# Value pages multiplied four at a time instead of two, with the loads, the v and u weights and the sample's scan products regrouped

## The chip, the core and the metric

The kernel runs on one core of a Trainium2 chip. The metric is the device time of one execution in microseconds (us). In the rows, PE is the matrix engine (TensorE), PEld its weight loads, DVE the vector engine, ACT the scalar engine, POOL GpSimd, SP the sync engine whose queue issues most of the loads.

## What is computed

One decoder layer for a prompt of 256 tokens and for 8 samples with one new token each, so 264 columns go through every product together. One projection `z = x @ w_in` feeds two mixers, differential attention and a diagonal state-space scan; their outputs are projected, gated, merged and go through `w_out`, a layer norm and a gated MLP. Cut to what the change touches:

```python
z = x @ w_in                          # q, k, v, u, gate_a, gate_s
k_past = cache_k[l][page_table].reshape(bs, n_pages * PAGE_SIZE, N_HEADS, 2, HEAD_DIM)
v_past = cache_v[l][page_table].reshape(bs, n_pages * PAGE_SIZE, N_HEADS, V_DIM)
...
s = jnp.einsum('bqhjd,bkhjd->bhjqk', q, k) * (HEAD_DIM ** -0.5)
p = jax.nn.softmax(s, axis=-1)
p_diff = p[:, :, 0] - lam * p[:, :, 1]
return jnp.einsum('bhqk,bkhe->bqhe', p_diff, v)
...
bu_re = jnp.einsum('blgc,gpc->blgp', ug, bb_re)      # scan inputs
y = jnp.einsum('blgp,gcp->blgc', x_re, c_re) - jnp.einsum('blgp,gcp->blgc', x_im, c_im)
```

Each sample has 2048 past tokens: 16 pages of keys and 16 of values, 128 tokens to a page, 512 KB each. With 8 samples this is 128 pages of each kind.

## The kernel before

All of `z` is made on PE as fp32 products, a 128 x 128 block of `w_in` against 264 columns (the matmul in `z_group`, L740). A tile of `z` is one bank of 128 outputs and takes 16 such matmuls; each shows as two records in the trace, so "x16" there is eight matmuls. Tiles q, k, v, u, g (gates) and glu follow the list `GROUPS`: most in pairs that share a load of 1 MB in rows of 1024 B, a few alone, in rows of 512 B. ACT issues these loads into a ring of four places and takes every finished tile from its bank (L1241).

Everything else of the attention and the scan is hung between those matmuls. There are seven *rounds* `i` = 0 to 6 that go over the tiles v, u and four g (round 6 has no u). A *quarter* is four matmuls of z; a round has 24 quarters (round 6 has 20), and the dictionary `at` names what PE does ahead of a quarter:

- `scores` (L858), `max_rows`, `global_max` (L896), `denominators` (L901), `combine` (L909), the transposes to rows (L689) and `prompt_pv` (L884, L885) are small products for the attention of prompt head `i` and sample `i`;
- `outputs_and_inputs` are the prompt's scan products `bu` (L832, 32-row tiles of the array) and `cx` (L843);
- `page_pv` (L720) multiplies one page of values: four matmuls with 16 columns of weights each, at four column groups of the array, against 256 columns of the page. Sixteen pages accumulate in one bank. In the kernel before they go two at a time (`pages_pv(i, 0, 1)` and so on), at quarters 2, 5, 10, 12, 15, 17, 20 and 23;
- `sample_bu` (L952) and `sample_cx` (L962) are the samples' scan products, 16 matmuls of 32 columns each.

For the keys, POOL multiplies each page with the query (L648), DVE reduces it (L1793); DVE also does maxima, the scan's states and the softmax parts. K pages have five places in memory, V pages four. SP issues the page loads, each after it has read the page's number (L453, L454), in the order of one list; it stops at a page whose place isn't free, with all that is behind it in the list.

`MAIL_ORDER` fixes the order in which small results pass from PE through one bank to ACT (`post` on PE, `take` on ACT). After the rounds come g 28 and 29, eight glu tiles and g 30 and 31, with sample 7's pages, the states' transposes and the mean squares of the norms in between. Then the weights of the remaining layers are split in two parts, high by ACT (L1487) and low by DVE (L1955), and multiplied as three products (L1083, L1084, L1089), first for the two branch projections and so on to the end. That part is not touched but for two waits.

## Time and profile before

| | |
|---|---|
| timed runs | 1684.76, 1690.97, 1694.06 us; median 1690.97 us |
| profiled execution | 1686.51 us, its span 1684.7 us |
| PE busy | 1642.8 us, 98% of the span |
| DVE, ACT, POOL busy | 1128.9, 647.8, 388.9 us |
| HBM traffic | 385.24 MB read, 5.46 MB written, 232 GB/s over the span |
| first projection product | 696.02 us after the start of the span |

The four middle rounds each take 61.80 us, round 5 (486.3 to 552.0 us) 65.7 us. In the rows an instruction's start and duration stand with its line; durations on PE overlap, since matmuls are pipelined, so what a run of matmuls costs is read from one start to the next. "[0.27 <-ACT ...]" is idle time before an instruction and what ended it.

### The profile page before, as it was taken

The page shows a single profiled execution, that of the slowest core. Times are in us where ns is not written, and L with a number is a line of the kernel's source. Part 1 is how long each engine was busy: PE and PEld are TensorE (multiplying, and loading weights), DVE is VectorE, ACT ScalarE, POOL GpSimd, SP SyncE. Part 2 cuts the span into 40 slices and gives each one's busy share as a digit, 9 for nine tenths or more (in the row PEclk, how much of TensorE's full clock was granted, in tenths as well). Part 3 has the DMA queues.
Part 4 walks back from the last instruction along what each step waited for, and adds up shares of the span by engine and source line. Part 5 has one row for each costly group of instructions (what it writes and reads, how often), then busy time and mean ns, then how long its engine had stood idle before and what let it go on. Part 6 is the DMA issues. An engine that isn't in the chain of part 4 may idle for free. (4 is left out here: it accounts for less than half of the span.)

```text
span 1684.7 us, 31240 instructions
## 1 busy us (share of the span) xinstructions
PE 1642.8 (98%) x11730; PEld 1466.0 (87%) x11730; DVE 1128.9 (67%) x1748; ACT 647.8 (38%) x979; POOL 388.9 (23%) x341
## 2 busy tenths in 40 slices
PE   9999999999999899899997999999999999999996
PEld 7878777777777676899997999999999999999995
DVE  2382897897888943777667767777777775545555
ACT  2121343443443322333347444444444443333333
POOL 1066587687677610000001000000000000000001
PEclk9999999999999999999998999999999999999998
DMA  9679899999999968666663676666766666666651
GB/s 251 213 229 312 285 392 387 388 394 386 388 392 394 327 230 260 166 182 180 186 177 99 186 192 173 178 179 180 192 174 176 182 178 168 183 180 179 183 152 53
DMA packets 484439, 391.81 MB, mean 233 GB/s; under 512 B 23550, under 2 KB 448411, under 8 KB 484316
## 3 DMA queue, kind: packets, MB, share of 16 engines
q1 hardware_dynamic: 401388, 323.27, 62.4%
q10 hardware_dynamic: 82944, 67.11, 12.8%
q8 instruction: 67, 1.10, 0.3%
q14 instruction: 40, 0.33, 0.1%
HBM read 385.24 MB, written 5.46 MB: 232 GB/s over the span
## 5 line engine op out<-in xcount | busy, mean ns | idle before, releaser
L740 PE MATMUL bank<-work,weight_ring 128*128 128x264 f32 x2176 | 518.2, 393 | 0.5 <-ACT work L1205 0.5
L1487 ACT ACTIVATE weights_hi<-weight_ring 128x2048 fp32r<-128x2048 f32 (+1 forms) x166 | 309.8, 1866 | 512.8 <-PE bank L1084 395.6
L740 PEld LDWEIGHTS bank<-work,weight_ring 128*128 128x128 f32 x2176 | 406.9, 192 | 91.3 <-issue 24.3
L1955 DVE TENSOR_TENSOR weights_lo<-weight_ring,weights_hi 128x2048 fp32r<-128x2048 f32 (+1 forms) x166 | 369.1, 2224 | 112.6 <-ACT weights_hi L1487 67.2
L1083 PE MATMUL bank<-h_hi,weights_hi 128*128 128x264 f32 x1344 | 330.9, 284 | 0.0
L1084 PE MATMUL bank<-h_lo,weights_hi 128*128 128x264 f32 x1344 | 330.1, 284 | 0.0
L648 POOL TENSOR_TENSOR work<-work 128x512 f32<-128x512 f32 x256 | 317.7, 1278 | 37.1 <-DMA work<-toeplitz_rows 20.7
L678 POOL TENSOR_TENSOR work<-work,ffn_scratch 128x1056 f32<-128x1056 f32 x4 | 9.5, 2406 | 1058.0 <-ACT ffn_scratch L1205 1058.0
L1083 PEld LDWEIGHTS bank<-h_hi,weights_hi 128*128 128x128 f32 x1344 | 253.2, 188 | 0.0
L1084 PEld LDWEIGHTS bank<-h_lo,weights_hi 128*128 128x128 f32 x1344 | 252.7, 188 | 0.0
L1793 DVE TENSOR_REDUCE work<-work 128x8 f32<-128x512 f32 x256 | 165.2, 677 | 52.6 <-POOL work L648 52.1
L1089 PE MATMUL bank<-h_hi,weights_lo 128*128 128x264 f32 x1344 | 176.5, 284 | 0.0
L1083 PE MATMUL bank<-hidden_hi,weights_hi 128*128 128x264 f32 x688 | 171.1, 286 | 1.8 <-DVE ffn_scratch L2083 1.8
L1084 PE MATMUL bank<-hidden_lo,weights_hi 128*128 128x264 f32 x688 | 170.7, 286 | 0.0
L1089 PEld LDWEIGHTS bank<-h_hi,weights_lo 128*128 128x128 f32 x1344 | 168.4, 188 | 0.0
L1205 ACT ACTIVATE work<-bank 128x264 f32<-128x264 f32 (+9 forms) x117 | 39.6, 352 | 263.4 <-PE bank L689 92.7
L1083 PEld LDWEIGHTS bank<-hidden_hi,weights_hi 128*128 128x128 f32 x688 | 130.6, 190 | 2.0 <-DVE ffn_scratch L2083 2.0
L1084 PEld LDWEIGHTS bank<-hidden_lo,weights_hi 128*128 128x128 f32 x688 | 130.5, 190 | 0.0
L2080 DVE SCALAR_TENSOR_TENSOR ffn_scratch<-bank,conv_and_ln_parameters,ffn_scratch 128x255 f32<-128x255 f32 x86 | 41.5, 483 | 126.4 <-ACT ffn_scratch L1205 126.4
L1089 PE MATMUL bank<-hidden_hi,weights_lo 128*128 128x264 f32 x688 | 91.4, 284 | 0.0
L1089 PEld LDWEIGHTS bank<-hidden_hi,weights_lo 128*128 128x128 f32 x688 | 86.7, 188 | 0.0
L637 POOL TENSOR_SCALAR work<-work 128x256 f32<-128x256 f32 x32 | 34.5, 1077 | 178.3 <-ACT work L1266 178.3
(272 smaller groups left out, 1939.5 us busy)
## 6 DMA issues: line engine op xcount, KB each, us to landing
weight_ring<-in_w_up SPq DMA_DIRECT2D x86, 1024.0 KB, 5.6
work<-in_cache_k SPq DMA_DIRECT2D x128, 512.0 KB, 7.0
work<-in_cache_v SPq DMA_DIRECT2D x128, 512.0 KB, 7.3
weight_ring<-in_w_in ACTq DMA_DIRECT2D x60, 1024.0 KB, 14.7
weight_ring<-in_w_down SPq DMA_DIRECT2D x32, 1024.0 KB, 5.9
weight_ring<-in_w_out SPq DMA_DIRECT2D x16, 1024.0 KB, 5.9
weight_ring<-in_w_down SPq DMA_DIRECT2D x16, 704.0 KB, 4.8
weight_ring<-in_w_proj_attn SPq DMA_DIRECT2D x16, 512.0 KB, 4.2
```

Of the source, the lines that this page charges most:

```text
L637: ch.did(pool.tensor_scalar(whole_turns, turns, 1.5 * 2 ** 23, -1.5 * 2 ** 23, ALU.add, ALU.add))
L648: pool.tensor_tensor(half_page(2 * n + e), half_page(2 * n + e), q_b[b % 2][:, e * 512:(e + 1) * 512], ALU.mult).then_inc(kq_ready, 1)
L678: pool.tensor_tensor(c3, c3, mean_y.unsqueeze(1).to_broadcast([P, 4, N]), ALU.subtract).then_inc(cent_ready, 1)
L740: last = pe.matmul(bank[(n + m) % 2][:, 0:N], chunk_weight(g, k - c * per, m), tiles[k], start=(k == 0), stop=(k == len(tiles) - 1))
L1083: pe.matmul(dst[:, 0:N], weight(w_hi, off, k0 + k), highs[k], start=start and k == 0, stop=False)
L1084: last = pe.matmul(dst[:, 0:N], weight(w_hi, off, k0 + k), lows[k], start=False, stop=False)
L1089: last = pe.matmul(dst[:, 0:N], weight(w_lo, off, k0 + k), highs[k], start=False, stop=stop and k == len(highs) - 1)
L1205: return act.activation(dst, src, ACT.Copy, scale=scale)
L1487: act.activation(w_hi[:, (j % 2) * KT * P:(j % 2) * KT * P + k_tiles * P].bitcast(F32R), slot3(j, 0, k_tiles).rearrange("p k m -> p (k m)" ...
L1793: dve.tensor_reduce(score[b % 3][:, p * 16 + 8 * e:p * 16 + 8 * e + 8], half_page(2 * n + e).rearrange("p (m d) -> p m d", d=HD), AX.X, AL ...
L1955: dve.tensor_tensor(w_lo[:, cols].bitcast(F32R), slot3(off % SLOTS, 0, k_tiles).rearrange("p k m -> p (k m)"), w_hi[:, cols], ALU.subtract ...
L2080: n1 = ch.did(dve.scalar_tensor_tensor(y[:, 1:T], ps[:, 0:T - 1], par(1), y[:, 1:T], ALU.mult, ALU.add))
```

## The change

Values: the 64 bursts of two pages become 32 of four, at quarters 10, 15, 20 and, in the next round, 4. SP's list is regrouped to match: V loads stand four together, K loads between them. `combine` moves from quarter 12, ahead of `denominators`, to behind the pages of quarter 15.

Weights: in rounds 0 to 5 the tiles v of two rounds make one pair and so do the tiles u, so twelve single loads become pairs; `v_t` gets a second place.

Samples: `sample_bu`, once 16 matmuls in one run at quarter 16 of round 6, goes in four parts of four matmuls at quarters 13 to 16, and `sample_cx`, once at quarter 1 after round 6, in four parts at quarters 17 to 20 of it, now into bank 4. DVE's mask of u and its read of the result move with them.

End of the input projection: `combine` of sample 7, the samples' mean square and the two transposes of states change places inside the last group, and PE's and DVE's waits before the first projection are split, so that g 31 is awaited only at the second product group and the stores only at the first merge.

```diff
+ROUNDS = []
+for _i in range(0, H - 2, 2):
+    ROUNDS += [[(("v", _i + 1), ("v", _i + 2)), (("u", _i + 2), ("u", _i + 3)), (("g", 4 * _i), ("g", 4 * _i + 1))],
+               in_pairs("g", 4 * _i + 2, 4 * _i + 8)]
+ROUNDS += [[(("v", H - 1),), *in_pairs("g", 4 * H - 8, 4 * H - 4)]]
...
-                for what in ("Sk", "P14", "P15", "V0", "K5", "V1", "K6", "Sv", "V2", "K7", "V3", "Bias", "K8", "Q", "V4", "K9",
-                             "V5", "K10", "V6", "K11", "V7", "V8", "K12", "V9", "K13", "V10", "K14", "V11", "K15", "V12",
-                             "N0", "N1", "V13", "N2", "N3", "N4"):
+                for what in ("Sk", "K5", "K6", "Sv", "V0", "V1", "V2", "V3", "K7", "Bias", "K8", "Q", "K9",
+                             "V4", "V5", "V6", "V7", "K10", "K11", "K12", "V8", "V9", "V10", "V11", "K13", "K14", "K15",
+                             "V12", "V13", "V14", "V15", "N0", "N1", "N2", "N3", "N4"):
...
-            def pages_pv(b, *numbers):
-                for p in numbers:
+            def pages_pv(b, first):
+                for p in range(first, first + 4):
                     if b >= 0:
                         page_pv(b, p)
...
-            def sample_bu():
-                pe.wait_ge(um_ready, 1)
-                pe.wait_ge(sc_read, 2 * (H - 1))
-                for t in range(HT):
+            def sample_bu(t0):
+                if t0 == 0:
+                    pe.wait_ge(um_ready, 1)
+                    pe.wait_ge(sc_read, 2 * (H - 1))
+                for t in range(t0, t0 + 2):
...
-                at = {2: lambda: (values_to_rows(i), pages_pv(i - 1, 12, 13)),
+                at = {2: lambda: values_to_rows(i),
                       3: lambda: max_rows(i),
-                      4: lambda: scores(i, 1, 1),
-                      5: lambda: (global_max(i), pages_pv(i - 1, 14, 15)),
+                      4: lambda: (scores(i, 1, 1), pages_pv(i - 1, 12)),
+                      5: lambda: global_max(i),
                       8: lambda: outputs_and_inputs(t, 0),
-                      10: lambda: (scores(i, 0, 0), pages_pv(i, 0, 1)),
+                      10: lambda: (scores(i, 0, 0), pages_pv(i, 0)),
                       12: lambda: diagonal_scores_and_sums(i)}
                 if whole:
-                    at |= {15: lambda: pages_pv(i, 4, 5),
-                           17: lambda: pages_pv(i, 6, 7),
-                           20: lambda: (pages_pv(i, 8, 9), outputs_and_inputs(t, 2)),
+                    at |= {15: lambda: (pages_pv(i, 4), combine_of(i - 1)),
+                           20: lambda: (pages_pv(i, 8), outputs_and_inputs(t, 2)),
                            21: lambda: p_diff_rows(i),
-                           23: lambda: (pages_pv(i, 10, 11), keys_to_rows(i + 1))}
+                           23: lambda: keys_to_rows(i + 1)}
                 else:
-                    at |= {14: lambda: pages_pv(i, 4, 5),
-                           16: lambda: (pages_pv(i, 6, 7), sample_bu()),
-                           18: lambda: pages_pv(i, 8, 9),
-                           20: lambda: (pages_pv(i, 10, 11), outputs_and_inputs(t, 2))}
+                    at |= {13: lambda: sample_bu(0),
+                           14: lambda: (pages_pv(i, 4), combine(i - 1), sample_bu(2)),
+                           15: lambda: sample_bu(4),
+                           16: lambda: sample_bu(6),
+                           17: lambda: sample_cx(0),
+                           18: lambda: (sample_cx(2), pages_pv(i, 8)),
+                           19: lambda: (p_diff_rows(i), sample_cx(4)),
+                           20: lambda: (sample_cx(6), outputs_and_inputs(t, 2), keys_to_rows(i + 1))}
+                z_groups(ROUNDS[i], at)
...
             z_group((("g", 30), ("g", 31)),
-                    {2: states_out, 4: sample_states_out, 5: lambda: combine(B - 1)})
-            pe.wait_ge(sq_ready, 2)
-            pe.matmul(bank[5][:, 0:H * B], v_mean_w[:, :], sq_sample, start=True, stop=True).then_inc(ms_done, 1)
+                    {1: lambda: combine(B - 1), 4: sample_mean_square, 5: states_out, 7: sample_states_out})
...
-            pe.wait_ge(z_read, PROJ0)
+            pe.wait_ge(z_read, PROJ0 - 1)
+            pe.wait_ge(mail_read, len(MAIL_ORDER))
```

How PE's order changes, in matmuls (line numbers of the changed kernel are one lower here). Before, on PE in the middle of a round, from the second scores product of quarter 10 on: L720 are pages, L740 is z, L909 `combine`, L901 `denominators`.

```order
L858 MATMUL bank<-work 128x128
L720 MATMUL bank<-work 16x256 x8
L740 MATMUL bank<-work,weight_ring 128x264 x8
L720 MATMUL bank<-work 16x256 x8
L858 MATMUL bank<-work 128x128
L909 MATMUL bank<-small,work 128x4 x2
L901 MATMUL bank<-work,ones 128x32
L740 MATMUL bank<-work,weight_ring 128x264 x12
L720 MATMUL bank<-work 16x256 x8
L740 MATMUL bank<-work,weight_ring 128x264 x8
L720 MATMUL bank<-work 16x256 x8
```

In the changed kernel the same stretch, pages on L719, z on L739, `combine` on L908, `denominators` on L900:

```order
L857 MATMUL bank<-work 128x128
L719 MATMUL bank<-work 16x256 x16
L739 MATMUL bank<-work,weight_ring 128x264 x8
L857 MATMUL bank<-work 128x128
L900 MATMUL bank<-work,ones 128x32
L739 MATMUL bank<-work,weight_ring 128x264 x12
L719 MATMUL bank<-work 16x256 x16
L908 MATMUL bank<-small,work 128x4 x2
L739 MATMUL bank<-work,weight_ring 128x264 x20
L719 MATMUL bank<-work 16x256 x16
```

Two bursts of eight page matmuls with z between have become one of sixteen, and `combine` has left the place ahead of `denominators` and stands behind the next pages.

PE in round 6 before, around `sample_bu` (L952):

```order
L740 MATMUL bank<-work,weight_ring 128x264 x8
L720 MATMUL bank<-work 16x256 x8
L740 MATMUL bank<-work,weight_ring 128x264 x8
L720 MATMUL bank<-work 16x256 x8
L952 MATMUL bank<-work 128x32 x16
L740 MATMUL bank<-work,weight_ring 128x264 x8
L720 MATMUL bank<-work 16x256 x8
L740 MATMUL bank<-work,weight_ring 128x264 x8
```

PE in round 6 of the changed kernel, `sample_bu` on L952 and `sample_cx` on L962:

```order
L739 MATMUL bank<-work,weight_ring 128x264 x4
L952 MATMUL bank<-work 128x32 x4
L739 MATMUL bank<-work,weight_ring 128x264 x4
L719 MATMUL bank<-work 16x256 x16
L908 MATMUL bank<-small,work 128x4 x2
L952 MATMUL bank<-work 128x32 x4
L739 MATMUL bank<-work,weight_ring 128x264 x4
L952 MATMUL bank<-work 128x32 x4
L739 MATMUL bank<-work,weight_ring 128x264 x4
L952 MATMUL bank<-work 128x32 x4
L739 MATMUL bank<-work,weight_ring 128x264 x4
L962 MATMUL bank<-work 128x32 x4
```

The run of 16 small matmuls has become four runs of four, each with z work of a quarter behind it; `sample_cx` follows in the same way.

PE in the last group before the projections (g 30, g 31), before: L689 the transposes of states, L1073 the samples' mean square, L1083 the first projection product.

```order
L740 MATMUL bank<-work,weight_ring 128x264 x8
L689 MATMUL bank<-ident,work 32x128 x2
L740 MATMUL bank<-work,weight_ring 128x264 x8
L689 MATMUL bank<-ident,work 128x128 x4
L740 MATMUL bank<-work,weight_ring 128x264 x4
L909 MATMUL bank<-small,work 128x4 x2
L740 MATMUL bank<-work,weight_ring 128x264 x12
L1073 MATMUL bank<-work,v_mean_w 128x64
L1083 MATMUL bank<-att_hi,weights_hi 128x264
```

The same in the changed kernel (L688, L908, L1071, L1084):

```order
L739 MATMUL bank<-work,weight_ring 128x264 x4
L908 MATMUL bank<-small,work 128x4 x2
L739 MATMUL bank<-work,weight_ring 128x264 x12
L1071 MATMUL bank<-work,v_mean_w 128x64
L739 MATMUL bank<-work,weight_ring 128x264 x4
L688 MATMUL bank<-ident,work 32x128 x2
L739 MATMUL bank<-work,weight_ring 128x264 x8
L688 MATMUL bank<-ident,work 128x128 x4
L739 MATMUL bank<-work,weight_ring 128x264 x4
L1084 MATMUL bank<-att_hi,weights_hi 128x264
```

The mean square now has three quarters of z and both transposes behind it; it was the last thing ahead of the projections.

## Rows read from the trace of the kernel before

**Rows 1.** The page: span; PE busy us and its share of the span

```profile
span 1684.7 us, 31240 instructions
...
PE 1642.8 (98%) x11730; PEld 1466.0 (87%) x11730; DVE 1128.9 (67%) x1748; ACT 647.8 (38%) x979; POOL 388.9 (23%) x341
```

**Rows 2.** By windows: busy us of PE, PEld, DVE, ACT, POOL; clock, DMA, GB/s

```profile
424.50:486.30 61.80, 61.53 (x381) 44.39 (x380) 51.34 (x86) 25.60 (x56) 46.73 (x41) 1.00 1.05 389
486.30:552.00 65.70, 61.69 (x381) 44.36 (x381) 55.27 (x84) 25.24 (x54) 45.37 (x40) 1.00 1.03 383
552.00:625.00 73.00, 70.47 (x429) 51.32 (x429) 46.01 (x81) 19.51 (x40) 34.81 (x29) 0.91 0.79 278
```

**Rows 3.** Timeline of PE, a round: start us, duration us, line, records

```profile
505.55 0.61 PE L909 MATMUL bank<-small,work 128*128 128x4 f32 x4
506.43 0.41 PE L901 MATMUL bank<-work,ones 128*128 128x32 f32 x2 [0.27 <-ACT work L1205]
...
512.19 1.06 PE L720 MATMUL bank<-work 128*16 128x256 f32 x16
513.18 3.83 PE L740 MATMUL bank<-work,weight_ring 128*128 128x264 f32 x16
516.93 1.06 PE L720 MATMUL bank<-work 128*16 128x256 f32 x16
517.92 5.61 PE L740 MATMUL bank<-work,weight_ring 128*128 128x264 f32 x24
...
536.79 3.73 PE L740 MATMUL bank<-work,weight_ring 128*128 128x264 f32 x16
540.35 0.38 PE L689 MATMUL bank<-ident,work 128*128 128x128 f32 x2
...
552.00 0.36 PE L896 MATMUL bank<-small,ones 16*128 16x16 f32 x2 [3.74 <-DVE small L1810]
```

**Rows 4.** Timeline of PE, around the sample's scan products

```profile
584.40 0.63 PE L720 MATMUL bank<-work 128*16 128x256 f32 x8 [0.57 <-DMA work<-in_cache_v]
584.95 4.67 PE L952 MATMUL bank<-work 128*128 128x32 f32 x32
589.44 6.26 PE L740 MATMUL bank<-work,weight_ring 128*128 128x264 f32 x16
...
607.45 3.66 PE L962 MATMUL bank<-work 128*128 128x32 f32 x32
610.94 3.35 PE L740 MATMUL bank<-work,weight_ring 128*128 128x264 f32 x8
```

**Rows 5.** By windows: PE's granted clock behind the first of them

```profile
588.00:594.00 6.00, 6.00 (x19) 4.97 (x19) 2.05 (x4) 0.00 (x0) 5.50 (x5) 0.50 0.97 394
```

**Rows 6.** Timeline of DVE before the first projection

```profile
682.08 2.29 DVE L1932 TENSOR_TENSOR att_lo<-work,att_hi 128x2048 fp32r<-128x2048 f32 x1
...
690.25 0.22 DVE L1942 TENSOR_TENSOR work<-work 128x64 f32<-128x64 f32 x1
```

**Rows 7.** Timeline of ACT there

```profile
690.66 1.89 ACT L1487 ACTIVATE weights_hi<-weight_ring 128x2048 fp32r<-128x2048 f32 x1
```

**Rows 8.** Timeline of PE: the first projection product

```profile
696.02 0.36 PE L1083 MATMUL bank<-att_hi,weights_hi 128*128 128x264 f32 x1 [4.24 <-DVE att_lo L1932]
```

**Rows 9.** DVE's groups in the fourth round, with idle time before them

```profile
L1793 DVE TENSOR_REDUCE work<-work 128x8 f32<-128x512 f32 x32 | 20.8, 678 | 7.6 <-POOL work L648 7.5
...
L1759 DVE SCALAR_TENSOR_TENSOR work<-bank,work 128x512 f32<-128x512 f32 (+1 forms) x2 | 1.1, 554 | 1.9 <-PE bank L858 1.9
```

**Rows 10.** Timeline of DVE: one long instruction

```profile
535.84 6.88 DVE L1799 TENSOR_TENSOR work<-work 128x256 f32<-128x256 f32 x1
```

**Rows 11.** Timeline of SP's DMA queue: two page loads issued

```profile
500.79 0.33 SPq L454 DMA_DIRECT2D work<-in_cache_v  x1
501.89 0.33 SPq L454 DMA_DIRECT2D work<-in_cache_k  x1
```

**Rows 12.** DMA issues, 499 to 520 us: KB each, median us to landing

```profile
work<-in_cache_v SPq DMA_DIRECT2D x7, 512.0 KB, 7.6
```

## Prediction on record

> **What bounds the kernel now.** I read the page first: PE is busy 1642.8 of 1684.7 us [rows 1], so time can only be won on PE, by fewer or cheaper instructions or by waits taken away. The change stands almost wholly in the part up to the first projection product at 696.02 us; behind it the weights' products follow as before. Then the windows: a middle round takes 61.80 us with PE busy for 61.53, while DVE has 51.34, ACT 25.60 and POOL 46.73 [rows 2]. The same windows show the second thing to watch: the DMA share is 1.05 at 389 GB/s, so the transfers have no visible room either. PE sets the round, but not by much. Round 5 is longer for one wait of PE of 3.74 us [rows 3], behind a DVE instruction that took 6.88 us [rows 10]; I have no reason to think that it comes from the order of the work, so the sum neither removes nor keeps it on purpose: it is in the profiled time that I start from, and its absence would be a gift of 3.7 us. Third, PE's timeline in a round gives the prices, fourth the clock behind the samples' scan products.
>
> **1. Fewer, longer page bursts.** Two pages together take 513.18 - 512.19 = 0.99 us from start to start [rows 3]; one page alone took 584.95 - 584.40 = 0.55 [rows 4]. So the second page costs 0.44, the entry 0.11, and four pages 0.99 + 2 x 0.44 = 1.87, where two bursts of two cost 1.98. The trace has no burst of four; the bounds are 1.76 (pages at the rate within, no entry at all) and 1.98 (nothing saved). I take 1.87, which is nearest to what a record within a burst costs: 32 merges x 0.11 = **3.5 us**.
>
> **2. Fewer changes between z and pages.** Sixteen records of z between two bursts took 516.93 - 513.18 = 3.75, and between other full-width products 540.35 - 536.79 = 3.56 [rows 3]: 0.19 for the two sides, 0.095 a side. This is on top of term 1, since it is read from the z run and not from the burst. By the order of PE, neighbours of z and pages fall from 80 to 34, since in the new order pages mostly stand beside scores, `combine` or `cx` on one side. 46 x 0.095 = **4.4 us**. If a side beside scores costs part of what one beside z does, less is won; the low bound is half, 2.2.
> A rule bears on it: the Trainium skill, TensorEngine Tiling (Array Packing), Tiling Modes, says that a change of the tiling mode, not of the tile alone, drains the engine. The trace agrees as far as it goes, with 0.095 a side. Counted by that rule, the changes of mode fall from 210 to 150, and 60 of them at 0.16 (0.095 on the z side and half of the entry of 0.11) would give 9.6 instead of the 7.9 of terms 1 and 2.
>
> **3. `combine` moved.** Seven times `denominators` waits for ACT to take `combine`'s result, [0.27 <-ACT] [rows 3]. With `combine` behind the next pages, ACT has two quarters or more. 7 x 0.27 = **1.9 us**. What is behind it in the mail order, `p_diff`, comes five quarters later, and finds ACT less than half busy.
>
> **4. The samples' scan products in parts.** The run of 32 records of L952 took 4.49 us, that of L962 3.49, and the z behind the first took 6.26 instead of 3.83 [rows 3, 4]. The granted clock was 0.50 there, that is 1.2 GHz instead of 2.4 [rows 5]. What PE did before it fell is a run of matmuls of 32 columns. Behind L962, eight z matmuls less took 3.35 where half of 3.83 is 1.9. So the clock cost 2.4 behind the first, about 1.4 behind the second, and 1.0 within the first (4.49 - 3.49). With four matmuls at a time and a quarter of z between, I expect the clock to stay at 1.00: 4.8. Against that stand six more entries; at 0.11 each, the dearest entry above, that is 0.7. **4.1 us**. Bounds: 0 if the clock still falls, 4.8 if entries are free. `sample_cx` now needs DVE's sum two us after the last `sample_bu` (quarter 16 to 17): DVE must reach it in its list, behind a page's reduction of 0.68 [rows 9]; a wait here would be about 1 us, which I leave to the range. All else in round 6 (73.0 us, PE 70.47 busy [rows 2]) only moves.
>
> **5. The first projection.** PE's own work ended at 696.02 - 4.24 = 691.8 [rows 8]; the wait was for the samples' columns: `combine` late in the group, DVE's sum at 690.25 [rows 6], square on ACT, mean square on PE, root on ACT, split on DVE. Now `combine` is at quarter 1, and DVE adds right behind the prompt's split, which ends at 682.08 + 2.29 = 684.4 [rows 6]. PE comes to the mean square at quarter 4, near 683.7, and waits about 1.2 there; so its z ends near 693.0. All of ACT's and DVE's part of the samples' norm fits into the three quarters behind. What is late next is ACT: its first high part of weights, 1.89 us [rows 7], stands in its list behind the copy of the sample states, whose transposes come one quarter (1.9) before the end. Allowing 1 us for copy and hand-over: 693.0 - 1.9 + 1.0 + 1.89 = 694.0, and the first product near 694.2. Gain 696.0 - 694.2 = **1.8 us**. Bounds: 0 (a later link of the same chain takes over) and 3 (all that lies between 696.0 and 693.0).
>
> **6. What it may cost.** V has four places. A burst of four frees them all at once, and SP issues four loads in a row, 501.89 - 500.79 = 1.10 us apart [rows 11]. The first goes out some 0.5 after the burst's start, the fourth 3.3 later, and it lands 7.6 after that [rows 12]: 11.4 after the burst began. The tightest interval is quarter 15 to 20: 1.87 for the burst, 2.5 x 3.75 of z, 0.3 of `combine`, 11.5; the fourth page is wanted 3 x 0.44 = 1.3 later, at 12.8. There is 1.4 us of room at the median landing, and the later half of the landings eats into it. There are about 7 such intervals at quarter 15 and 7 at quarter 10. Before, with V and K in turn, PE waited 0.57 for a page once [rows 4]. I put 0.15 us on each of these 14: **-2.0 us**. The K loads stand behind the V loads in SP's list and now wait for four at once; DVE has 7.6 us of waiting for POOL in a round [rows 9] and PE doesn't wait for page sums at once, so nothing on the path. ACT evicts the same tiles in another order, under z. The pairs of v and u move the same bytes in larger rows; the trace does not price it apart. I take 0; it can only help or leave the share of 1.05 as it is, except as rival A has it.
>
> **The sum.** 3.5 + 4.4 + 1.9 + 4.1 + 1.8 - 2.0 = 13.7. From the profiled 1686.5: 1672.8. The median of the runs shown is 4.5 above the profiled run, so a median may come out at 1673 to 1677; I say **1674**.
>
> **Rivals.**
> A (slower): **the value loads starve PE.** Eight loads that once went out alternately, V and K, now go as bursts onto queues already at a share of 1.05. For it: the room of 1.4 us is 18% of the landing time. Against: V and K before were nearly as dense, and landed in 7.6. From a landing of 9.0 on, every burst at quarters 15 and 20, and soon 10 and 4, waits. At 10.5 the wait is 1.5 in each of 21 (the first of each sample has longer), 31 us: 1674 + 2 + 31 = 1707; it ends slower than now from 0.8 us a burst on, 17 us. Time 1690 to 1700.
> A rule speaks for A: the Trainium skill, DMA: Bandwidth & Descriptors, Queues, rings and completion order, says that each DMA engine takes turns between its queues by the packet. By it larger rows on ACT's queue would take a larger part beside the pages, and these would land later while a v or u pair loads. No row here shows a page beside rows of either size apart.
> B: **DMA or the key chain becomes the bound.** PE's round would be 61.8 - 4 x 0.11 - 6 x 0.095 - 0.27, that is 60.5. DVE without its wait for scores of 1.9 [rows 9] needs 59.9, so it just fits. The transfers would have to go from 389 to 397 GB/s. If they can't, the rounds stay at 61.8 and terms 1 to 3 are lost but for their part outside the six rounds: 9.8 x 0.75 = 7.4 less, 1681. PE would then wait for pages or scores in rounds where it didn't.
> C: **the clock falls all the same** in round 6, and the projection starts as before: 5.9 less, 1680. For it: the parts of four are still followed by a page burst at two places. Against: such bursts are all over the rounds, at clock 1.00 [rows 2].
> D: terms 1 and 2 mean nothing (the drain is hidden under weight loads): 7.9 less, 1682. Against it stand the two intervals of rows 3.
>
> **How the numbers follow.** Chances: forecast (1667 to 1679) 0.58, A 0.12, B 0.13, C 0.08, D 0.06, better than 1667 (no long instruction on DVE, loads ease) 0.03. A measurement here tells about 0.5% from nothing, 8.5 us: faster is below 1682.5. The forecast, C, most of B, half of D and the better case are faster: but runs of this kernel spread over 9 us, which moves a third of B, C and D across. Faster 0.69; A ends half within 0.5% and half slower, with a little for what I don't see: same 0.23, slower 0.08. The range holds the forecast, B, C and D, 1663 to 1686; its ends take in the bounds: terms 1, 2 and 4 at their best give 3 to 5 more, at their worst 9 less.
>
> **What would show it.** A burst on L719 (32 records) of 1.85 to 1.90 from start to start. Rounds of 60.5 to 60.8. No wait at L900 for ACT. Clock 1.00 behind the parts of L952 and L962. The first product of L1084 some 13.7 us earlier than before, near 682.3. Waits of PE for `in_cache_v` of under 3 us together; if they are over 15, A holds. If PE's rounds stay at 61.8 with PE idle, B; if they do with PE busy, D. The forecast is wrong if any of the three comes.

## The result: slower, by 1.1%

The changed kernel took 1701.13 us (median of 7 runs, 1696.68 to 1709.68), the kernel before 1684.76 us beside it (7 runs, 1679.38 to 1694.06). The ratio is 1.0109, with a 95% interval of 1.008 to 1.0137. I had forecast 1674 us, 11 under the 1684.76 measured beside it; instead 16 were lost.

The page of the changed kernel, span and busy times, as [rows 1]:

```profile
span 1707.9 us, 31242 instructions
...
PE 1651.5 (97%) x11730; PEld 1476.4 (86%) x11730; DVE 1121.3 (66%) x1748; ACT 649.3 (38%) x981; POOL 388.1 (23%) x341
```

This profiled execution is the longest of the seven. Some 5 of the 23 us that it has over [rows 1] arise from 0 to 60 us, at a clock of 0.91 and 0.83 in two windows of 20 us, in a part that the change does not touch. The rest arises in the rounds: at round 0's global maximum it is 6 us behind (185.1 against 179.2), at the first projection product 25 (720.95 against 696.02). Four of them, from one global maximum to the next, by windows (columns as in [rows 2]):

```profile
245.50:310.50 65.00, 60.99 (x382) 44.59 (x381) 49.45 (x84) 25.41 (x54) 45.37 (x40) 1.00 1.00 369
310.50:375.80 65.30, 63.24 (x380) 45.99 (x381) 50.71 (x86) 25.63 (x56) 46.56 (x41) 0.97 0.99 362
375.80:443.60 67.80, 64.90 (x381) 47.06 (x380) 50.83 (x86) 25.41 (x54) 46.72 (x41) 0.95 0.98 357
443.60:509.90 66.30, 61.66 (x382) 44.79 (x381) 50.67 (x86) 25.53 (x56) 46.52 (x41) 1.00 1.01 367
```

A round takes 65 to 68 us where it took 61.80 [rows 2]. PE's busy share has fallen, so PE waits; and in two of the four its clock was below 1.00. The transfers moved 357 to 369 GB/s in place of 389, at a DMA share of still 0.98 to 1.01, so the share doesn't tell whether they are the bound. What PE waited for in the whole run:

```profile
PE bank L719 <- DMA work<-in_cache_v: 10.2, 12, 1.1
...
PE bank L895 <- DVE small L1815: 8.3, 3, 4.0
PE bank L962 <- DVE work L1888: 3.6, 1, 3.6
...
PE bank L1071 <- ACT work L1480: 1.3, 1, 1.3
```

L719 are the pages, L895 the global maximum, L962 the samples' outputs, L1071 the mean square. PE's timeline in the third of these rounds:

```profile
388.98 1.92 PE L719 MATMUL bank<-work 128*16 128x256 f32 x32
390.83 3.83 PE L739 MATMUL bank<-work,weight_ring 128*128 128x264 f32 x16
394.59 0.49 PE L857 MATMUL bank<-work 64*128 64x128 f32 x2
...
400.77 0.62 PE L719 MATMUL bank<-work 128*16 128x256 f32 x8
401.82 0.63 PE L719 MATMUL bank<-work 128*16 128x256 f32 x8 [0.43 <-DMA work<-in_cache_v]
403.50 0.62 PE L719 MATMUL bank<-work 128*16 128x256 f32 x8 [1.05 <-DMA work<-in_cache_v]
405.13 0.98 PE L719 MATMUL bank<-work 128*16 128x256 f32 x8 [1.01 <-DMA work<-in_cache_v]
406.04 1.02 PE L908 MATMUL bank<-small,work 128*128 128x4 f32 x4
406.91 11.70 PE L739 MATMUL bank<-work,weight_ring 128*128 128x264 f32 x40
418.54 1.92 PE L719 MATMUL bank<-work 128*16 128x256 f32 x32
```

The burst of quarter 10 takes 1.85 from start to start, as forecast. The next one falls into four single pages, of which the last three wait for their loads. Behind it stands `combine` (L908), later by all of that, and behind `combine` 40 records of z take 418.54 - 406.91 = 11.63 us where two and a half runs of 16 at 3.75 make 9.4: the clock.

```profile
402.00:404.00 2.00, 0.95 (x16) 0.13 (x8) 0.00 (x0) 0.00 (x0) 0.00 (x0) 1.00 1.03 409
...
408.00:412.00 4.00, 4.00 (x11) 3.07 (x10) 0.69 (x1) 0.91 (x5) 3.92 (x4) 0.50 1.04 396
```

It was 1.00 while PE waited, 0.50 (1.2 of 2.4 GHz) from 408 to 412 us, right behind 2.5 us of idle time in 4.4, and 0.99 from 412 to 416. Here the wait is paid twice. It isn't always: the same burst waited 1.9 us in the first of the four rounds, 2.1 in the second and 2.1 in the fourth, and the 40 records of z behind it took 9.15, 10.83 and 9.15 us. In two of the four rounds the clock held.

The page loads from 250 to 480 us, KB each and median us to landing:

```profile
work<-in_cache_v SPq DMA_DIRECT2D x56, 512.0 KB, 9.2
work<-in_cache_k SPq DMA_DIRECT2D x55, 512.0 KB, 9.1
```

9.2 us where the row of before was 7.6 [rows 12], and 7.3 over the same window. I had put 1.4 us of room there. The loads that the burst above waited for, from 390 to 395 us, were slower still:

```profile
390.38 3.63 SPq L459 DMA_DIRECT2D work<-in_cache_v  x4
```

```profile
work<-in_cache_v SPq DMA_DIRECT2D x4, 512.0 KB, 10.6
```

What I had not looked at is ACT and POOL. ACT's timeline of the kernel before, at the same place of its third middle round: it takes `combine` (L1205, 8 columns, 382.58) and goes on to the scan's turns (L1266), a table of 256 columns that POOL works on next, once the z tile of 386.91 is out.

```profile
382.58 0.18 ACT L1205 ACTIVATE work<-bank 128x8 f32<-128x8 f32 x1 [7.66 <-PE bank L909]
...
386.91 0.39 ACT L1241 ACTIVATE work<-bank 128x264 f32<-128x264 f32 x1 [2.15 <-PE bank L740]
...
387.45 0.51 ACT L1266 ACTIVATE work<-work,conv_and_ln_parameters 128x256 f32<-128x256 f32 x1
```

POOL there, waiting for the turns:

```profile
388.04 1.07 POOL L637 TENSOR_SCALAR work<-work 128x256 f32<-128x256 f32 x1 [10.00 <-ACT work L1266]
```

And in the changed kernel, ACT first, then POOL, which waits for those turns (L636) before it can multiply the next key page, and what DVE waited in this round for such pages:

```profile
399.09 0.39 ACT L1245 ACTIVATE work<-bank 128x264 f32<-128x264 f32 x1 [2.15 <-PE bank L739]
...
407.09 0.18 ACT L1209 ACTIVATE work<-bank 128x8 f32<-128x8 f32 x1 [7.60 <-PE bank L908]
...
407.26 0.50 ACT L1270 ACTIVATE work<-work,conv_and_ln_parameters 128x256 f32<-128x256 f32 x1
```

```profile
407.84 1.07 POOL L636 TENSOR_SCALAR work<-work 128x256 f32<-128x256 f32 x1 [15.57 <-ACT work L1270]
```

```profile
DVE work L1798 <- POOL work L647: 15.4, 10, 10.4
```

The turns could have gone out at 399.5, behind the tile of 399.09. ACT stands still for 7.60 us, since `combined` is ahead of them in its list and `combine` on PE stands behind the pages. POOL idles for 15.57 in place of 10.00, and DVE for 15.4 in place of 7.5 [rows 9]. With a period of 59.9 by my own count DVE has no 8 us to give: the page sums, the maximum over all pages (L1815) and PE's L895 come late.

### The profile page after: what moved, and what is told of

Same layout as the page of the kernel before. It is cut to its first block and busy times, and to the rows that moved or that the text cites. A ratio compares the mean times of both kernels' runs of the same rounds, so it can differ in the third digit from the quotient of the medians.

```text
span 1707.9 us, 31242 instructions
## 1 busy us (share of the span) xinstructions
PE 1651.5 (97%) x11730; PEld 1476.4 (86%) x11730; DVE 1121.3 (66%) x1748; ACT 649.3 (38%) x981; POOL 388.1 (23%) x341
## 5 line engine op out<-in xcount | busy, mean ns | idle before, releaser
L739 PE MATMUL bank<-work,weight_ring 128*128 128x264 f32 x2176 | 527.3, 398 | 3.1 <-DMA weight_ring<-in_w_in 2.0
L739 PEld LDWEIGHTS bank<-work,weight_ring 128*128 128x128 f32 x2176 | 413.8, 195 | 88.3 <-issue 17.2
L1084 PE MATMUL bank<-h_hi,weights_hi 128*128 128x264 f32 x1344 | 331.0, 284 | 0.0
L1084 PEld LDWEIGHTS bank<-h_hi,weights_hi 128*128 128x128 f32 x1344 | 253.2, 188 | 0.0
L1084 PE MATMUL bank<-hidden_hi,weights_hi 128*128 128x264 f32 x688 | 169.7, 284 | 1.8 <-DVE ffn_scratch L2095 1.8
L1209 ACT ACTIVATE work<-bank 128x264 f32<-128x264 f32 (+8 forms) x117 | 40.1, 354 | 287.2 <-PE bank L739 106.7
L1084 PEld LDWEIGHTS bank<-hidden_hi,weights_hi 128*128 128x128 f32 x688 | 129.5, 188 | 2.0 <-DVE ffn_scratch L2095 2.0
L719 PE MATMUL bank<-work 128*16 128x256 f32 x1024 | 66.3, 390 | 10.9 <-DMA work<-in_cache_v 10.2
```

What stands on the lines that cost most here:

```text
L719: last = pe.matmul(bank[5][32 * g:32 * g + 16, 0:2 * P], score[b % 3][:, p * 16:(p + 1) * 16], page(v_pages, n)[:, g * 2 * P:(g + 1) * 2 * ...
L739: last = pe.matmul(bank[(n + m) % 2][:, 0:N], chunk_weight(g, k - c * per, m), tiles[k], start=(k == 0), stop=(k == len(tiles) - 1))
L1084: pe.matmul(dst[:, 0:N], weight(w_hi, off, k0 + k), highs[k], start=start and k == 0, stop=False)
L1209: return act.activation(dst, src, ACT.Copy, scale=scale)
```

## Experiments

All times are medians; ratios are against runs of the kernel before on the same chip. Experiments 1 to 4 ran on one chip, 5 to 8 on a second and 9 to 12 on a third, so across these groups the ratios are compared and not the times. Waits and rounds are those of one profiled execution each.

**1. The old list of loads.** `e1_old_list` differs from the changed kernel in SP's order alone (the lines that load V14 and V15 a round later come back with it, not shown):

```diff
-                for what in ("Sk", "K5", "K6", "Sv", "V0", "V1", "V2", "V3", "K7", "Bias", "K8", "Q", "K9",
-                             "V4", "V5", "V6", "V7", "K10", "K11", "K12", "V8", "V9", "V10", "V11", "K13", "K14", "K15",
-                             "V12", "V13", "V14", "V15", "N0", "N1", "N2", "N3", "N4"):
+                for what in ("Sk", "P14", "P15", "V0", "K5", "V1", "K6", "Sv", "V2", "K7", "V3", "Bias", "K8", "Q", "V4", "K9",
+                             "V5", "K10", "V6", "K11", "V7", "V8", "K12", "V9", "K13", "V10", "K14", "V11", "K15", "V12",
+                             "N0", "N1", "V13", "N2", "N3", "N4"):
...
```

> The changed kernel, but with the order of SP's page loads of the kernel before (V and K in turn); the bursts of four pages stay. Theory 1 (the grouped loads are at fault: four values in a row at 1.1 us each pile up on the queue, values and keys land in 9 to 10 us instead of 7, and next sample's first keys stand behind V12 to V15): landings go back to 7 to 8 us, and most of the loss is won back, 1684 to 1690 us. Theory 2 (the bursts themselves are at fault: they free four places at once, so the fourth load is always late, whatever the list says): PE still waits for values, 10 us or more in all, and the time stays at 1695 to 1705. Theory 3 (the larger rows of v and u push the pages back): landings stay at 9 to 10 us, 1700.

1737.0 us, ratio 1.0317 (1.0287 to 1.0347).

```profile
PE bank L725 <- DMA work<-in_cache_v: 51.6, 28, 3.1
```

The landings went back (6.9 us), the time did not: with V and K in turn the later values of a burst wait in SP's list for a key's place (sample 4's V10 had its place free at 492.3 us and went out at 504.7), and PE waits 51.6 us for values. Theory 1 falls: the grouped list is what a burst of four needs, not what is wrong. Theory 2 had the wait right and its size far too low. Theory 3 had the landings wrong.

**2. Next keys between V12 to V15.** `e2_keys_between`:

```diff
-                             "V12", "V13", "V14", "V15", "N0", "N1", "N2", "N3", "N4"):
+                             "N0", "V12", "N1", "V13", "N2", "V14", "N3", "V15", "N4"):
```

> The changed kernel with one stretch of SP's list changed: the next sample's first five keys stand between V12 to V15 (N0, V12, N1, V13, ...) and not behind them. Theory 1a (the chain of the keys sets the round: the first key of the next sample goes out 3.6 us after its place is free, where before it was 0.8): rounds shorten by 2 to 3 us, PE's waits for the global maximum fall from 8 us to under 2, about 1688. Theory 1b (the values' own landings set it): the global maximum's waits go, the waits for values stay at 10 us, and the time falls by under 6 us, 1695 or more.

1707.18 us, 1.0133 (1.0109 to 1.0157). The waits for the global maximum went, those for values rose to 25.2 us; the time is that of the changed kernel or a little over. The delay is real but only changes its place; neither form of theory 1 explains the loss.

**3. v and u alone.** `e3_single_rows` loads each of these tiles by itself, in the changed order:

```diff
-    ROUNDS += [[(("v", _i + 1), ("v", _i + 2)), (("u", _i + 2), ("u", _i + 3)), (("g", 4 * _i), ("g", 4 * _i + 1))],
+    ROUNDS += [[(("v", _i + 1),), (("v", _i + 2),), (("u", _i + 2),), (("u", _i + 3),), (("g", 4 * _i), ("g", 4 * _i + 1))],
```

> The changed kernel with the v and u tiles loaded alone (rows of 512 B) in the changed kernel's order of tiles. Theory 3 (larger rows on ACT's queue push the pages back): pages land in about 7.5 us again and the time falls to 1685 to 1690. Theories 1 and 2: nothing to do with the rows, landings stay at 9 to 10 us, and the time is 1698 to 1706, rather slower for the packets that come back.

1705.04 us, 1.0124 (1.01 to 1.0149): no difference to the changed kernel, so the larger rows are not the cause of the loss. They do something: PE's waits for values were 4.5 us and not 10.2, and the values' median landing 8.0 and not 9.2 from 250 to 480 us (7.7 and 8.1 from 185 to 550). The wait went elsewhere, to the global maximum, 15.1 us and not 8.3.

**4. The old pages.** `e4_old_pages` puts the values back to two at a time at their eight places, with the old list; all else of the change stays. (Diff, not shown: the lines on pages in `at` and in the groups behind the rounds, and the list, turned back.)

> The changed kernel with the value pages two at a time at the eight places of the kernel before and with its list of loads; combine's place, the pairs of v and u, the sample's scan products in parts and the new end stay. If the pages and their loads are the whole loss, this has only what I forecast for the other parts: combine 1.9, scan products 4.1, projection start 1.8, so about 8 us under the kernel before, 1674 to 1679. If it isn't faster than the kernel before, one of these terms is wrong too, or the pairs of v and u cost something: then 1684 or more.

1679.8 us, 0.9994 (0.9972 to 1.0017). So without the bursts the loss is gone, but the 8 us that I gave to the other parts are not there. Its waits show where they went:

```profile
PE bank L901 <- DVE small L1824: 3.2, 5, 1.2
PE bank L725 <- DMA work<-in_cache_v: 2.5, 5, 0.8
...
PE bank L968 <- DVE work L1897: 1.8, 1, 1.8
```

Its rounds take 62.9 us, 1.1 more than before. Something other than the bursts makes DVE late, by waits of PE up to 1.2 us (L901 is the global maximum here). DVE's longest wait for POOL was 5.7 us and not 3.7, and POOL's for the turns behind `combined`, ACT's copy of `combine`'s result, 11.4 and not 10.3. Counted from the round's global maximum, ACT started these turns at 449.25 - 424.51 = 24.7 us in the kernel before and at 454.26 - 427.19 = 27.1 here:

```profile
454.09 0.18 ACT L1218 ACTIVATE work<-bank 128x8 f32<-128x8 f32 x1 [2.91 <-PE bank L914]
...
454.26 0.50 ACT L1279 ACTIVATE work<-work,conv_and_ln_parameters 128x256 f32<-128x256 f32 x1
```

That pointed to `combined` in ACT's list.

**5. ACT takes `combine` behind the turns, old pages.** `e5_copy_behind_turns` is experiment 4 with

```diff
-                if i:
+                if i and not whole:
                     combined(i - 1)
                 final_states(4 * t + 2)
                 if t + 1 < HT:
                     turns(4 * t + 4)
+                if i and whole:
+                    combined(i - 1)
```

> The kernel of the fourth experiment (changed kernel with the old value pages), with one move in ACT's list: in rounds 1 to 5 ACT takes combine's result behind the scan turns, on which POOL waits, and not ahead of them. Theory A (combine at quarter 15 holds ACT, so POOL gets its turns 1.4 us later, DVE the eighth page 2 us later, and the round is 62.9 instead of 61.8): the rounds go to 61.3 to 61.6, the wait of DVE for POOL back under 4 us, and the sample scan's wait of 1.8 for DVE shrinks; 6 to 9 us under the fourth experiment, 8 to 11 us under the kernel before. Theory B (the pairs of v and u, or their evictions, set 62.9): no change against the fourth experiment.

1675.65 us, 0.9945 (0.992 to 0.9969), by the ratios half a per cent under experiment 4. Three of the rounds take 61.4 to 61.9 (another two 64 and more, one of them with a DVE instruction of 6.9 us), DVE's longest wait for POOL is 2.8, and PE's wait in round 6 fell from 1.8 to 0.4. Theory A holds.

**6. The same move with the bursts.** `e6_same_with_bursts` is the changed kernel with those lines and nothing else.

> The changed kernel with the same move in ACT's list and nothing else; bursts of four and the new list stay. Theory A as the whole cause: the waits for the global maximum (8 us) go, and the time comes to the kernel before or under it. Theory C (two causes: ACT's place and the bursts' transfers): the waits for the global maximum and for the sample scan's states go, those for value pages stay at 10 us or grow, rounds 63 to 65, and the time is 6 to 12 us over the kernel before, about half of the loss.

1676.04 us, 0.9962 (0.994 to 0.9983). One small copy moved in ACT's list gives back 1.5% of the time: from 1.1% slower to 0.4% faster.

```profile
PE bank L719 <- DMA work<-in_cache_v: 6.4, 11, 1.1
```

```profile
388.35 0.39 ACT L1245 ACTIVATE work<-bank 128x264 f32<-128x264 f32 x1 [2.14 <-PE bank L739]
...
388.89 0.51 ACT L1270 ACTIVATE work<-work,conv_and_ln_parameters 128x256 f32<-128x256 f32 x1
393.24 0.19 ACT L1209 ACTIVATE work<-bank 128x8 f32<-128x8 f32 x1 [3.83 <-PE bank L908]
```

The waits for the global maximum are gone. The turns leave at 388.89, right behind the tile of 388.35, and `combine` is taken at 393.24 with nothing of POOL's behind it. Theory A came; theory C, 6 to 12 us over the kernel before, did not. The waits for values fell too, from 10.2 to 6.4, so part of the starvation came with the late keys. SP's own waits fit a way for it: a key load whose place DVE hasn't freed holds the values behind it in SP's list. From 240 to 490 us SP waited 51.0 us for DVE in the kernel before, 92.8 in the changed one and 71.9 here. No run tests that link by itself.

**7. `combine` alone.** `e7_combine_alone` is the kernel before with `combine` moved on PE, in `MAIL_ORDER` and on ACT. ACT's lines:

```diff
...
-                if i:
-                    combined(i - 1)
                 sums_copy(i)
                 if whole:
                     evict(tiles[2])
+                if i:
+                    combined(i - 1)
```

> The kernel before with combine alone moved to behind the pages of quarter 15 (on PE, in the mail order and in ACT's list, as in the change). Theory A: rounds grow by 1 to 1.5 us though the wait of 0.27 is gone, and the time is 4 to 8 us over the kernel before. My forecast's step 3: 1.9 us under it. Theory B: 1 to 2 us under it.

1692.92 us, 1.0052 (1.0028 to 1.0076), and rounds of 62.6 and more where they were 61.8. The move that I had booked with a gain of 1.9 us costs 0.5% by itself, a little more than theory A's 4 to 8 us. It starves PE of values as well, with the old pages and the old list: 7.5 us of such waits where the kernel before had 0.6, and SP waited 64.9 us for DVE from 240 to 490 us, not 51.0.

**8. Values by half.** `e8_half_values` is experiment 6 with half of each value page from the fifth on; it leaves out the other half, and its place keeps what was there:

```diff
-                load_page(cv, n, page(v_pages, n), v_in[n % 4])
+                if n < 4:
+                    load_page(cv, n, page(v_pages, n), v_in[n % 4])
+                else:
+                    load_page(cv[:, :, 0:512], n, page(v_pages, n)[:, 0:512], v_in[n % 4])
```

> The sixth experiment's kernel, but each value page from the fifth on is loaded by half (256 KB, its first 512 columns; the other half keeps what was there), so the output differs. Theory C (the values' transfers starve the bursts): PE's waits for values fall from 10 us to under 1, rounds to 60.5 to 61.2 (what I forecast for the bursts), the time 12 to 17 us under the kernel before. If PE's waits go but rounds stay over 61.8, the bursts have no gain of their own; if DVE's waits for POOL stay, the keys' chain is the bound without any transfer.

1667.63 us, 0.9901 (0.9869 to 0.9933).

```profile
238.50:298.80 60.30, 60.30 (x382) 44.83 (x381) 50.88 (x88) 26.62 (x55) 47.61 (x42) 1.00 0.95 329
...
419.50:479.80 60.30, 60.30 (x382) 44.84 (x381) 51.08 (x86) 25.91 (x57) 46.79 (x41) 1.00 0.95 331
```

Rounds of 60.3 us, with PE busy in all of them and the clock at 1.00. This is what the moves in the rounds are worth to PE when their values are there: 1.5 a round, where steps 1 to 3 said 1.3. The 0.6% between this and experiment 6 is about what the full transfers still cost. The wait at the first part of `sample_cx` is not of that kind: it was 3.8 us here, with no burst waiting for a value.

**9. DVE's sum earlier.** `e9_sum_earlier` is experiment 6 with the sum of the samples' states ahead of `map_weights` and one page reduction:

```diff
                 reduce_page(b, 10)
+                if i == H - 2:
+                    dve.wait_ge(bs_done, HT // 2)
+                    dve.tensor_tensor(xs_new...).then_inc(xn_ready, 1)
                 map_weights(i)
                 reduce_page(b, 11)
-                if i == H - 2:
-                    dve.wait_ge(bs_done, HT // 2)
-                    dve.tensor_tensor(xs_new...).then_inc(xn_ready, 1)
```

> The sixth experiment's kernel (bursts, ACT's list mended) with DVE's sum of the samples' states one page reduction and map_weights earlier in round 6. If the wait of PE at the first part of the samples' outputs (2.5 us) stands only for DVE's place, it falls to 0.6 and the time by 2 us against the sixth experiment. If DVE must wait for the last input part, nothing changes.

1674.05 us, 0.9944 (0.9923 to 0.9964). The wait at L962 stayed at 2.6 in the profiled run. DVE's sum did come earlier, 15.2 us behind the first part of `sample_bu` (590.26 - 575.04) and not 16.5 (589.39 - 572.90). PE came earlier by as much, since the burst of quarter 14 waited 1.15 us for a value in experiment 6 and not at all here. Inconclusive on what the place is worth; the time can't be told from experiment 6.

**10. `combine` alone, mended.** `e10_combine_mended` is experiment 7 with ACT's lines of experiment 5.

> The seventh experiment's kernel (kernel before with combine alone moved), with ACT taking combine's result behind the scan turns in rounds 1 to 5. If ACT's place was the whole cost of the move, the seventh's loss of 0.5% goes and my step 3 is left: 0 to 2 us under the kernel before, rounds 61.5. If the rounds stay over 62.5, it is the place on PE that costs.

1684.53 us, 1.0009 (0.9985 to 1.0033). The loss of experiment 7 is gone, PE's waits for values are 1.1 us and not 7.5, SP's for DVE 44.5, and four of the rounds take 61.4, 0.4 less than before. One round of the profiled run took 67.8, with a wait of 3.3 us for ACT (L884) and the clock behind it; whether such a round belongs to the kernel or to the run is open. The place on ACT was the cost, not that on PE.

**11. v and u alone, mended.** `e11_single_mended` is experiment 6 with the edit of experiment 3.

> The sixth experiment's kernel with the v and u tiles loaded alone again (rows of 512 B). If the larger rows push the pages back, PE's waits for values fall from 6 us to 3 or less and the time by 2 to 4 us. If they do nothing or relieve the transfers, the time is the same or up to 5 us more, with waits for values of 6 us or more.

1687.97 us, 1.0021 (0.9998 to 1.0044), against 0.9962 for experiment 6 on another chip and 0.9944 for experiment 9, which is experiment 6 but for DVE's sum, on this one. Neither branch of the expectation came: PE's waits for values were lower with single rows, 3.4 us here and 6.4 there, as in experiment 3, and yet the time is 0.6% longer. So the larger rows may delay the pages a little, and as a whole they help once ACT is mended; the gain isn't in the waits for values. Two rounds of the profiled run took over 67 us, with waits for ACT of 2.6 and 4.1; how the rows lead to that, I haven't shown.

**12. Bursts evenly apart.** `e12_even_bursts` is experiment 9 with

```diff
-                    at |= {15: lambda: (pages_pv(i, 4), combine_of(i - 1)),
-                           20: lambda: (pages_pv(i, 8), outputs_and_inputs(t, 2)),
+                    at |= {16: lambda: (pages_pv(i, 4), combine_of(i - 1)),
+                           20: lambda: outputs_and_inputs(t, 2),
                            21: lambda: p_diff_rows(i),
+                           22: lambda: pages_pv(i, 8),
...
-                             "V12", "V13", "V14", "V15", "N0", "N1", "N2", "N3", "N4"):
+                             "N0", "N1", "V12", "V13", "N2", "V14", "N3", "V15", "N4"):
```

> The ninth experiment's kernel with the bursts of rounds 0 to 5 evenly apart (quarters 4, 10, 16, 22 and not 4, 10, 15, 20) and the next sample's keys between V12 to V15. If the short intervals of five quarters are what the value loads miss, PE's waits for values fall from 6 us to under 2, and the time by 4 to 6 us, to 13 us under the kernel before. If the transfers as a whole are short, the waits only move to another burst or to the keys, and the time stays within 3 us.

1676.56 us, 0.9948 (0.9928 to 0.9967). PE's waits for values were 4.3 us in place of 6.5; the time is the same, and a wait of 4.8 us for DVE stands at the transposes (L688) of the profiled run. The waits moved, as the second branch of the expectation has it. The best versions that load whole pages are 5, 6, 9 and 12, all 0.4 to 0.6% under the kernel before and not told apart from each other.

## Why the forecast was wrong

**Step 1 was right, and steps 1 to 3 together in their sum.** A burst of four takes 1.85 us (forecast 1.87). z between a burst and scores takes 394.59 - 390.83 = 3.76, as between two bursts (3.75), so a side beside scores costs what one beside pages does, and step 2's account of sides is wrong in detail. But the round as a whole went to 60.3 in experiment 8, PE's busy time from 61.53 to 60.30, and my steps gave 60.5. No kernel that loads whole pages reached it in every round.

**Step 3 is the one that failed**, in the sentence "What is behind it in the mail order, `p_diff`, comes five quarters later, and finds ACT less than half busy." I looked at what is behind `combine` in the mail and at ACT's busy share, and not at what is behind it in ACT's own list: the scan's turns, for which POOL waits, for which DVE waits, for which the global maximum on PE waits. The step put this cost at nothing. As made, the move costs 0.5% (experiment 7); mended, about nothing (10). With the bursts it cost 1.5% (the changed kernel against 6), because `combine` also stood behind a burst that itself waited for its pages.

**Step 4 was half right.** Behind the parts of `sample_bu` the z matmuls ran at full clock (eight records in 2.03). But of the wait for DVE at the first part of `sample_cx`, which "I leave to the range" at about 1 us, this came:

```profile
614.34 2.03 PE L739 MATMUL bank<-work,weight_ring 128*128 128x264 f32 x8
619.93 1.60 PE L962 MATMUL bank<-work 128*128 128x32 f32 x8 [3.56 <-DVE work L1888]
621.34 3.87 PE L739 MATMUL bank<-work,weight_ring 128*128 128x264 f32 x8
625.00 1.75 PE L962 MATMUL bank<-work 128*128 128x32 f32 x8
626.69 3.62 PE L719 MATMUL bank<-work 128*16 128x256 f32 x32
```

3.56 us, and behind it half clock: z took 3.87 and not 2.03, the burst 3.62 and not 1.92, the two parts 1.60 and 1.75 and not 0.97. In all 3.6 + 1.8 + 1.7 + 1.4 = 8.5 us, more than the 4.8 that the parts save. With the old pages and ACT mended the wait is 0.4 (experiment 5). What a wait here costs beyond its length differs from run to run. In experiment 6 it was 2.53, and the clock held:

```profile
590.12 1.08 PE L962 MATMUL bank<-work 128*128 128x32 f32 x8 [2.53 <-DVE work L1890]
591.04 2.03 PE L739 MATMUL bank<-work,weight_ring 128*128 128x264 f32 x8
```

In experiment 4 it was 1.83, and z behind it took 2.91; in experiment 8 it was 3.76, and z took 3.87.

**Step 5 was right.** From the first z of the last group to the first projection product it took 721.0 - 702.9 = 18.1 us; before, 696.0 - 676.1 = 19.9. The mean square waited 1.3 (forecast 1.2), the gain is the 1.8 of the forecast.

**Step 6 was mis-sized.** -2.0 us stood for value waits of 10.2 us, plus the clock that fell behind some of them. It took the landing time of a kernel whose loads were spaced by their places, 7.6 us, for one that issues four to seven back to back; it was 9.2 in the median and 10.6 for the four loads of 390 to 395 us. And it put the first load 0.5 us behind the burst's start, where it goes out 1.4 behind it: 390.38 - 388.98 in the changed kernel, and in the kernel before 500.79 [rows 11] - 499.40:

```profile
499.40 1.06 PE L720 MATMUL bank<-work 128*16 128x256 f32 x16
```

So the room was 0.5 and not 1.4 even at the old landing time. With 1.4 + 3.3 + 10.6 = 15.3 against the 12.8 at which the fourth page was wanted, the estimate is 2.5 us late; the three waits of that burst make 2.49.

**The sum's last step** had no ground either: I added 1.2 us to 1672.8 since the median of the runs shown lay above the profiled one, and the median of the seven, 1684.76, lies below it.

**The rivals.** A (the loads starve PE) names a wait that is there, and its time is the one that came nearest, 1690 to 1700; its cause is only a part: it alone, in experiment 6, leaves the kernel faster than before. With smaller rows on ACT's queue the time is the same or longer (3, 11). The Trainium skill's rule that I put beside this rival (DMA: Bandwidth & Descriptors, Queues, rings and completion order) may hold: PE's waits for values were lower with the smaller rows both times, 4.5 against 10.2 us and 3.4 against 6.4, in one profile each. That larger rows cost the kernel time, these runs don't show. B (DMA or the key chain becomes the bound) had the place right, and the size wrong: it compared DVE's period of 59.9 with 60.5 and took for granted that DVE would be served as before. What I took as a bound that is met or not met is a chain through four engines in which each position in a list counts. None of my three signs of a wrong forecast came as I wrote it: the waits for values were 10.2 us, between 3 and 15, and the rounds stood at 65 to 68 us, not at 61.8. The signs that did fail were the rounds of 60.5 to 60.8, the clock behind the parts of L962, and the first product of L1084, at 720.95 and not near 682.3.

What stays open: how much of the value waits is left without any late keys (in experiment 6 POOL still waited 22.4 us for key pages from 240 to 490 us, in the changed kernel 13.0), what makes DVE late at the first part of `sample_cx`, and why the pairs of v and u help once ACT is mended.

## What to carry to other kernels

When an operation moves to a later place on one engine, read the list of the engine that takes its result: everything behind the taking waits too, and the busy share of that engine says nothing about it. Here one copy of 8 columns, ahead of a table that GpSimd needed, cost 1.5% together with the bursts and 0.5% without them. When an operation is put behind a burst that may wait for a transfer, it inherits that wait, and so do all who wait for it. And a wait on TensorE of a few us can cost more than its length, so price it from the rows behind such waits: here 3.56 us cost 8.5, while 2.53 us at the same place of experiment 6 cost no more than themselves.

## What the runs showed of the hardware

DVE instructions of a few hundred ns can take as long as POOL's own beside them. In round 6 of experiment 6, POOL multiplied without a break and four DVE instructions took 1.29 to 1.44 us:

```profile
581.18 1.44 DVE L1778 TENSOR_SCALAR work<-work,small 128x256 f32<-128x256 f32 x1
582.54 1.29 DVE L1779 TENSOR_SCALAR work<-work,small 128x128 f32<-128x128 f32 x1
583.87 1.39 DVE L1781 SCALAR_TENSOR_TENSOR work<-work,small 128x256 f32<-128x256 f32 x1
585.17 1.35 DVE L1783 SCALAR_TENSOR_TENSOR work<-work,small 128x128 f32<-128x128 f32 x1
```

```profile
579.98 7.67 POOL L647 TENSOR_TENSOR work<-work 128x512 f32<-128x512 f32 x6 [5.49 <-DMA work<-in_cache_k]
```

In the kernel before, the four took 1.4 us in all, and the first of them 0.34 at 585.11 us, just where an instruction of POOL ended and none followed for 2.7 us. POOL's six took 1.28 each. By this DVE was some 4 us later in that round, which may be part of PE's wait of 2.5 us there; I saw it and did not test it.

The other is the price of idling: the 2.5 us of waits in one burst were followed by 4 us or more at half clock, and the wait of 3.56 us by some 10 us, up to 630 us, in which most groups of PE took longer than at full clock. The length of the wait alone doesn't tell it: 1.83 us in experiment 4 were followed by slower matmuls, 2.53 in experiment 6 and 2.60 in experiment 9 at the same place were not.
